# Hybrid decoder block on one core: the mixer's normalised input kept on chip as high and low halves, every mixer projection in three float32r products

## Reference

```python
h = rmsnorm(x, norm_mix_g)
q, k, v, xr, yr, ga, gl = split_cols(h @ w_in)      # 512,128,128,512,512,1024,1024 columns
y_attn = sliding_window_attention(rope(q), rope(k), v, sinks) @ w_attn_o    # window 128, 8 blocks
xr = causal_depthwise_conv(xr, conv_w, conv_b)
y_lru = (rg_lru(xr, ...) * gelu(yr)) @ w_lru_o      # recurrence over positions
x = x + (sigmoid(ga) * y_attn + sigmoid(gl) * y_lru) @ w_out
h = rmsnorm(x, norm_ffn_g)
x = x + moe(h, ...)                                 # top 4 of 32 experts, clamped SwiGLU
return rmsnorm(x, norm_final_g)
```

## Time and profile before

| what | us |
|---|---|
| median of 3 runs | 2228.98 (2228.72 to 2231.96) |
| the profiled execution, and its span | 2230.49, 2228.9 |
| first branch product / last | 26.4 / 136.5 |
| block-diagonal products until | 150.3 |
| attention's project(3) starts | 211.4 |
| gates and projections | 353.5 to 641.7 |
| first product of w_out | 648.9 |
| experts' loop | from about 810 |

### The profile page before, as it was taken

One profiled execution on the slowest core, in us unless ns is written; L12 is line 12 of the kernel. 1 busy time (PEld: TensorE's weight loads), 2 busy tenths in 40 slices (PEclk: granted clock), 3 DMA queues, 4 the chain that ended last, 5 costly groups with the idle time before them and its releaser, 6 DMA issues.

```text
span 2228.9 us, 36027 instructions
## 1 busy us (share of the span) xinstructions
PE 2088.0 (94%) x11352; PEld 1494.9 (67%) x11353; DVE 1550.9 (70%) x1964; ACT 1244.1 (56%) x1655; POOL 291.4 (13%) x334
## 2 busy tenths in 40 slices
PE   7989988999989749999999999999999999999993
PEld 4445555767668637777777777777777777777772
DVE  4326654555443448878877778987877998977894
ACT  3152434334333336766766657766766776765674
POOL 3010000000002420211212200111210110220000
PEclk9998999999999869999999999999999999999997
DMA  7110020110143476988988779978979979977994
GB/s 225 38 38 0 22 76 1 38 39 1 38 151 133 142 196 224 371 284 287 377 282 282 256 260 380 373 270 291 370 259 325 372 276 368 356 258 246 378 342 159
DMA packets 247678, 489.51 MB, mean 220 GB/s; under 512 B 19915, under 2 KB 29991, under 8 KB 247536
## 3 DMA queue, kind: packets, MB, share of 16 engines
q1 hardware_dynamic: 218768, 439.37, 54.7%
q0 software_dynamic: 21088, 49.35, 8.4%
q10 hardware_dynamic: 7776, 0.19, 0.2%
HBM read 461.01 MB, written 32.05 MB: 221 GB/s over the span
## 4 chain that ended last, share of the span: by engine, by line
PE 84%; DVE 5%; issue 4%; ACT 2%; DMA 2%; SPq 1%; POOL 0%; ACTq 0%; DVEq 0%; POOLq 0%
PE psum L650 14%; PE psum L651 14%; PE psum L654 14%; PE psum L667 8%; PE psum L423 5%; PE psum L548 5%; PE psum L536 3%; PE psum L538 3%; PE psum L531 3%; PE psum L638 2%; PE psum L447 2%; PE psum L491 2%; PE psum L593 1%; PE psum L617 1%; PE psum L594 1%
## 5 line engine op out<-in xcount | busy, mean ns | idle before, releaser
L1451 DVE TENSOR_TENSOR w_lo<-ring,w_hi 128x1024 fp32r<-128x1024 f32 x768 | 915.0, 1221 | 144.2 <-ACT w_hi L890 132.7
L890 ACT ACTIVATE w_hi<-ring 128x1024 fp32r<-128x1024 f32 x768 | 803.7, 1059 | 277.7 <-PE psum L654 269.0
L650 PE MATMUL psum<-w_hi,rows_hi 128*128 128x512 f32 x1024 | 422.6, 413 | 4.3 <-DVE rows_lo L1455 2.5
L651 PE MATMUL psum<-w_hi,rows_lo 128*128 128x512 f32 x1024 | 400.4, 391 | 0.0
L654 PE MATMUL psum<-w_lo,rows_hi 128*128 128x512 f32 x1024 | 316.6, 390 | 0.0
L650 PEld LDWEIGHTS psum<-w_hi,rows_hi 128*128 128x128 f32 x1024 | 194.1, 190 | 47.0 <-issue 10.5
L654 PEld LDWEIGHTS psum<-w_lo,rows_hi 128*128 128x128 f32 x1024 | 192.7, 188 | 41.3
L650 PE MATMUL psum<-w_hi,act_hi 128*128 128x512 f32 x512 | 219.9, 429 | 0.0
L651 PEld LDWEIGHTS psum<-w_hi,rows_lo 128*128 128x128 f32 x1024 | 193.5, 189 | 37.7
L651 PE MATMUL psum<-w_hi,act_lo 128*128 128x512 f32 x512 | 202.7, 396 | 0.0
L667 PE MATMUL psum<-ring,region_m 128*32 128x256 f32 x3072 | 174.2, 380 | 0.0
(11 more groups left out here) (286 smaller groups left out, 2596.0 us busy)
## 6 DMA issues: line engine op xcount, KB each, us to landing
ring<-in_w_gate_up_dram SPq DMA_DIRECT2D x128, 2048.0 KB, 15.9
ring<-in_w_down_dram SPq DMA_DIRECT2D x64, 2048.0 KB, 12.0
ring<-in_w_in_dram SPq DMA_DIRECT2D x9, 1024.0 KB, 8.2
ring<-in_w_in_dram SPq DMA_DIRECT2D x3, 2048.0 KB, 22.6
region_m<-in_x_dram SPq DMA_DIRECT2D x8, 512.0 KB, 9.7
ring<-in_w_out_dram SPq DMA_DIRECT2D x2, 2048.0 KB, 7.7
region_a<-in_x_dram POOLq DMA_DIRECT2D x8, 512.0 KB, 4.8
acc_rows<-region_a POOLq DMA_DIRECT2D x8, 512.0 KB, 2.9
```

Of the source, the lines that this page charges most:

```text
L650: mm(bank(i), hi[:, ks], wh, start=(k0 + q == 0), stop=False)
L651: mm(bank(i), lo[:, ks], wh, start=False, stop=False)
L890: act.activation(w_hi[:, n % NBUF, :], place[i][:, k0 * HALF:(k0 + 2) * HALF], ACT.Copy).then_inc(hi_done, 1)
L1451: v.tensor_tensor(out=w_lo[:, n % NBUF, :], in0=place[i][:, k0 * HALF:(k0 + 2) * HALF], in1=w_hi[:, n % NBUF, :].bitcast(f32), op=ALU.subt ...
```

## The change

The mixer is rebuilt up to w_out; the experts' part and its weights' places stay.

- The input is kept as hT_hi (a ScalarE copy to float32r from the transposes' banks) and hT_lo (a VectorE subtraction), without the norm's gain; the gain goes into the weights, which are also split: ScalarE copies with a scale (`in_high`), VectorE multiplies and subtracts (`in_low`).
- Branches, q, k, v and the two output projections are three float32r products each (`three`).
- x is loaded in two halves with the first branch weights between. TensorE starts the branches after four tiles and does one group between each two of the other tiles' transposes. The groups' order is by token half first.
- ScalarE's 13 constant loads stand behind the eighth tile, and before the first copies out of the branch banks.
- Weights for k and v are loaded when eight branch groups are done, those for q when sixteen are, gates two groups ahead.
- The decay moves into step 1 of the attention loop on both engines, the recurrences into steps 1 and 2. The attention's output oT now lies on `igate`, so ScalarE waits for all recurrences before its first copy of pT. kT goes round four blocks.
- In the gates hT needs no splitting. In the projections oT and lruT are split in 16 pieces of 512 tokens for each group (`out_high`, `out_low`), in `OBUF` = 3 buffers.
- `bias_part` moves into the w_out steps 1 to 5, its loads behind the last projection.

```diff
 # sync
-            sp.dma_start(wq_sb, ...).then_inc(wq_in, 16)
-            sp.dma_start(wkv_sb, ...).then_inc(wkv_in, 16)
-            sp.wait_ge(branch_mm, 8)
+            tiles(0, NT // 2)
             sp.dma_start(wxr_sb, w_in_v[:, :, OFF_XR:OFF_XR + LW]).then_inc(wxr_in, 16)
+            tiles(NT // 2, NT)
             sp.dma_start(wyr_sb, w_in_v[:, :, OFF_YR:OFF_YR + LW]).then_inc(wyr_in, 16)
+            sp.wait_ge(branch_mm, 8)
+            sp.dma_start(wkv_sb, w_in_v[:, :, OFF_KV:OFF_KV + 2 * KVW]).then_inc(wkv_in, 16)
+            sp.wait_ge(branch_mm, 16)
             sp.dma_start(wq_sb, w_in_v[:, :, OFF_Q:OFF_Q + QW]).then_inc(wq_in, 16)
...
 # tensor
+            def three(dst, w_hi_, w_lo_, m_hi_, m_lo_, first, final):
+                mm(dst, w_hi_, m_hi_, start=first, stop=False)
+                mm(dst, w_hi_, m_lo_, start=False, stop=False)
+                return mm(dst, w_lo_, m_hi_, start=False, stop=final)
+
+            def branch(n):
+                w, m, th = n // 8, n % 4, n // 4 % 2
+                hi, lo = ((wxr_hi, wxr_lo), (wyr_hi, wyr_lo))[w]
+                if m == 0 and w == 0:
+                    pe.wait_ge(hT_lo_done, 4 * (th + 1))
+                if n >= 4:
+                    pe.wait_ge(branch_out, n - 3)
+                cols, toks = slice(m * P, (m + 1) * P), slice(th * HALF, (th + 1) * HALF)
+                for k in range(KD):
+                    if n % 8 == 0:
+                        pe.wait_ge(in_lo_done, w * KD + k + 1)
+                    last = three(bank(4 + n % 4), hi[:, k, cols], lo[:, k, cols], hT_hi[:, k, toks], hT_lo[:, k, toks],
+                                 k == 0, k == KD - 1)
+                last.then_inc(branch_mm, 1)
+
+            for t in range(NT // 2):
+                turn_x(t)
+            for t in range(NT // 2, NT):
+                branch(t - NT // 2)
+                turn_x(t)
+            for n in range(4, 16):
+                branch(n)
...
+                    three(bank(1)[:, 0:2 * KVW], h_, l_, wkv_hi[:, k, :], wkv_lo[:, k, :], k == 0, k == KD - 1)
...
+                    last = three(bank(0), h_, l_, wide[0], wide[1], k == 0, k == KD - 1)
...
+                    for q in range(2):
+                        cols = slice(q * P, (q + 1) * P)
+                        for th in range(2):
+                            mm(bank(2 * th + q), hi[:, cols], hT_hi[:, k, th * HALF:(th + 1) * HALF], start=first, stop=False)
...
-                for th in range(2):
-                    for q, (w, x_) in enumerate(((wao_sb, oT), (wlo_sb, lruT))):
-                        for k in range(GROUP):
-                            last = mm(bank(4 + 2 * th + q), w[:, k, j * P:(j + 1) * P], x_[:, k, th * HALF:(th + 1) * HALF],
+                for k in range(GROUP):
+                    for q in range(2):
+                        r = (j * GROUP + k) * 2 + q
+                        lo = (wao_lo, wlo_lo)[q][:, k, j * P:(j + 1) * P]
+                        for th in range(2):
+                            p_ = 2 * r + th
+                            pe.wait_ge(o_lo_done, p_ + 1)
+                            last = three(bank(4 + 2 * th + q), ow_hi[r % 2], lo, o_hi[p_ % OBUF], o_lo[p_ % OBUF],
+                                         k == 0, k == GROUP - 1)
+                            last.then_inc(o_mm, 1)
...
 # scalar
+            for t in range(NT // 2):
+                square(t)
+                if t >= 1:
+                    hT_high(t - 1)
+            hT_high(NT // 2 - 1)
+            act.wait_ge(gmix_in, 16)
+            in_high(wxr_hi, wxr_sb, wxr_in)
+            for t in range(NT // 2, NT):
+                square(t)
+                hT_high(t)
             with nc.allow_non_contiguous_dma("small vectors, one element per partition"):
                 for dst, src in loads:
                     act.dma_start(dst, src).then_inc(consts_in, 16)
+            for n in range(4):
+                branch_copy(n)
+            in_high(wyr_hi, wyr_sb, wyr_in)
...
+                if s == 1:
+                    decay()
                 if s >= 2:
                     b = s - 2
+                    if b == 0:
+                        act.wait_ge(lru_done, LM)
...
+            def out_high(p_):
+                r, th = p_ // 2, p_ % 2
+                j, k, q = r // 8, r // 2 % 4, r % 2
+                if p_ >= OBUF:
+                    act.wait_ge(o_mm, p_ - OBUF + 1)
+                if th == 0:
...
+                    act.activation(ow_hi[r % 2], (wao_sb, wlo_sb)[q][:, k, j * P:(j + 1) * P], ACT.Copy)
+                act.activation(o_hi[p_ % OBUF], (oT, lruT)[q][:, k, th * HALF:(th + 1) * HALF], ACT.Copy).then_inc(o_hi_done, 1)
...
+                for p_ in range(16 * j, 16 * j + OBUF):
+                    out_high(p_)
+                act.wait_ge(gate_mm, KD * (j + 1))
...
+                for p_ in range(16 * j + OBUF, 16 * (j + 1)):
+                    if p_ == 16 * j + 14 and j + 1 < KD:
+                        gate_high((j + 1) * KD)
+                        gate_high((j + 1) * KD + 1)
+                    out_high(p_)
 # vector
+            def out_low(p_):
...
+                    v.tensor_tensor(out=(wao_lo, wlo_lo)[q][:, k, cols], in0=(wao_sb, wlo_sb)[q][:, k, cols],
+                                    in1=ow_hi[r % 2].bitcast(f32), op=ALU.subtract)
+                v.tensor_tensor(out=o_lo[p_ % OBUF], in0=(oT, lruT)[q][:, k, th * HALF:(th + 1) * HALF],
+                                in1=o_hi[p_ % OBUF].bitcast(f32), op=ALU.subtract).then_inc(o_lo_done, 1)
...
-                if s < LM:
-                    recur(s)
+                if s == 1:
+                    decay()
+                    recur(0)
+                    recur(1)
+                if s == 2:
+                    recur(2)
+                    recur(3)
                 if s >= 1:
                     b = s - 1
...
                 if t + 2 < NT:
                     merged_low(t + 2)
+                if 1 <= t <= 5:
+                    bias_part(t - 1)
```

More of the change, by code:

```diff
@@ L30 @@
 FILL = 16
+OBUF = 3
 FAR = 4096
@@ L164, in hybrid_decoder_block, with pieces @@
         pT = take(2 * GROUP * P)
+        bd = pT.rearrange("p (g m n) -> p g m n", g=2, m=LM)
+        cos, sin = (take(NT * 32).rearrange("p (t d) -> p t d", t=NT) for _ in range(2))
+        squares, ang, turn = region_a[:, 0:D], unit_view(region_a[:, D:D + NT * 32], NT), unit_view(region_a[:, D + NT * 32:D + 2 * NT * 32], NT)
+        a2 = prob[0].rearrange("p h k -> p (h k)")
         at[0] = 0
         sgate = [[take(HALF) for _ in range(2)] for _ in range(2)]
[L168 to L183, removed]
+        def pieces(name, count, width):
+            col = at[0]
+            take(count * width)
+            return [over(f"{name}{n}", [P, width], at_a, col + n * width)[:] for n in range(count)]
+        g_hi = pieces("g_hi", 2, 2 * P)
+        o_hi, o_lo = pieces("o_hi", OBUF, HALF), pieces("o_lo", OBUF, HALF)
+        ow_hi = pieces("ow_hi", 2, P)
+        bstage = half_slot(4, 2)[:, 0:3 * D]
+        wo_lo = [over(f"wo_lo{q}", [P, UNIT], at_ring, (4 + q) * UNIT) for q in range(2)]
+        wo_hi = [over(f"wo_hi{q}", [P, UNIT], at_ring, (6 + q) * UNIT) for q in range(2)]
         m_hi = [over(f"m_hi{q}", [P, KD, P], at_s, 1536 + q * D) for q in range(2)]
@@ new lines, in _ @@
+            hT_low(NT // 2 - 1)
+            in_low(wxr_lo, wxr_sb, wxr_hi)
+            for t in range(NT // 2, NT):
+                xnorm(t)
+                hT_low(t)
+            dve.wait_ge(small_built, N_BUILT)
+            dve.wait_ge(consts_in, 16 * N_CONST)
+            then(v.tensor_scalar(clam[:, 2, :], lam[:], -1.0, None, ALU.mult))
+            v.tensor_tensor(out=clam[:, 0, :], in0=lam[:], in1=clam[:, 2, :], op=ALU.max).then_inc(clam_exp, 1)
+            in_low(wyr_lo, wyr_sb, wyr_hi)
@@ new lines, in _, with conv @@
+            then(v.memset(xr[:, :, 0:3], 0.0))
+            def conv(m):
+                dve.wait_ge(branch_out, 5 + m)
+                then(v.tensor_scalar(xc[:, m, :], xr[:, m, 3:3 + SEQ], convw[:, 3, m:m + 1], convb[:, m:m + 1], ALU.mult, ALU.add))
+                for c in (2, 1, 0):
+                    ins = v.scalar_tensor_tensor(out=xc[:, m, :], in0=xr[:, m, c:c + SEQ], scalar=convw[:, c, m:m + 1],
+                                                 in1=xc[:, m, :], op0=ALU.mult, op1=ALU.add)
+                    if c:
+                        then(ins)
+                    else:
+                        ins.then_inc(conv_done, 1)
```

347 lines of the change are left out of this document (167 added, 180 removed).

## The result

The changed kernel takes 2247.77 us (median of 4 runs, 2247.03 to 2248.79), the kernel before beside it 2228.85 (4 runs, 2228.14 to 2231.96): ratio 1.0082, 95% interval 1.0065 to 1.01. It is slower by 0.8%, where 0.6% was forecast; the forecast of 2243.2 is 4.6 us short, and the time lies inside its range. The profiled execution has a span of 2246.2 us.

A forecast was written before the change was run, and what follows sets the result against it. TensorE, busy 94% of the span, was taken as the bound; -0.6 us at the gates' start and +14.9 after gave +14.2, so 2243.2 us from a median of 2228.98, range 2222 to 2264.

The forecast's parts named there:

- Price of a product: Float32r products on TensorE: 0.231 us each, three cost 0.69 against 0.86 for one float32; k and v products 0.12.
- The relief of some 60 us: TensorE over the mixer: cheaper products relieve it of some 60 us in all, including 21.6 for the projections.
- Rival B: Branches, q and gates: a product takes 0.216 as two neighbours share weights; -16 us, 2227; chance 8%.
- Up to the branches: Start to branches' end: branch(0) begins at 22.6, branch(4) at 60.8, branches end at 129.2 instead of 136.5.
- The term of the constant loads: Before branch(4): TensorE waits behind 13 issues on ScalarE's queue, taken as 9 us; the other end is 22.
- rival C: Constant loads keep 22 us (+13), or k and v products cost 0.231 (+18): 2256 to 2261; chance 12%.
- Into the attention: Attention's start: VectorE's serial chain makes project(3) 10.0 us late; five blocks give 10.6 back; gates begin at 352.9.
- Gates: Gates of each column group: the copy and subtraction dropped were covered, so nothing is gained; 21.8 us remain.
- Projections: Output projections, fed by ScalarE and VectorE through 3 buffers: 15.6 against 13.73 us a group, +14.9 for the stage.
- the walk: Projections: all 16 pieces followed through the feed loop, with a 1.7 us wait behind the sigmoids, giving 15.6 us.
- Rivals A and D: Projections: A, feed loop closes at TensorE's pace, 12.7 a group, 2220, 10%; D, TensorE's clock falls, group 20.5, 2293, 8%.
- After: W_out stage: halving unchanged, bias work moved into half-idle VectorE steps costs nothing; 1 to 3 us if cover failed.

The follow-up runs named there:

- loads_early: Changed kernel with ScalarE's 13 constant loads issued in groups of 5, 5 and 3 behind tiles 4, 5 and 6: 2238.64 us, ratio 1.0032.
- gates_hi_w: Changed kernel with the third product of each gate step on high weights, so all load high halves; only gates read: 22.40 us a group.
- gates_lo_w: Changed kernel with all three products of each gate step loading low weights; only gates read: 21.77 us a group.

## Why the prediction came out as it did
- **Price of a product.** 0.231 was taken. The branches show 0.227 (the dense stretch from 69 to 126 us), k and v 0.12 as estimated, the projections' runs without a wait 0.23. A block takes 19.41 us against 19.27 worked out. Rival B's 0.216 did not come: neighbours with the same weights in the gates took 0.232. The Trainium skill ("TensorE: Matmul & The Clock Gate", Back-to-back issue gap) gives 216 ns as the gap of an isolated product; no dense stretch of float32r products here was that fast, the least being 0.227. The relief of some 60 us that was counted does not show in full: TensorE's busy time fell by 36.6. In the gates and projections it fell only from 286.2 to 284.0 us, where 21.6 had been counted, since a group's gates take 0.49 more and its projections are recorded busy 13.0 us, not the 11.1 of 48 products at 0.231.
- **Up to the branches.** branch(0) at 22.54 (22.6). The term of the constant loads was 7.9 us of issues instead of 9, and the block-diagonal products began 2.9 us before the 129.2 of the prediction; loads_early gives the term's share in the end, 7.0. The other end, 22 us, for which rival C stood, did not come. The prediction's reason was that the issues of the kernel before ran beside the weight loads. The rows agree in part: its slow ones, 2.92 to 3.46 us, stood where the DMA moved 341 to 387 GB/s, and here it moved 5 to 34. But three of its issues took only 0.38 to 0.78 between 18.35 and 20.24, where the DMA already moved 396, and no run tells what made the others slow.
- **Into the attention.** Each link of VectorE's chain has the length that was worked out: decay 10.2, recurrences 9.4 and 9.4, softmax 9.85, rotation 3.0. project(3) was 2.6 us earlier than predicted only because the chain began that much earlier. From there to the gates 8.7 came back instead of 10.6: the five blocks gave some 10 (19.41 us each instead of 21.40), and the stretch behind them took about 1 longer. So the forecast of the gates' start, right within 0.7 us, owes that to two misses against each other.
- **Gates.** This is the term that was mis-sized: "nothing is gained, 21.8 us remain". They took 413.99 - 391.69 = 22.3 us, 0.232 a product against 0.227 in the earlier trace rows, at the same granted clock of 1.00. Seven full groups make 3.4 us, more than the whole 2.4 that the forecast was short at the head of w_out (16.6 against 14.2); the stages before it were 0.7 better, and the start of this one 0.7. The other 2.2 of the 4.6 us between the medians lie behind (0.7 behind the head of w_out) and in the runs' own spread.
- **Projections.** 15.6 predicted, 15.63 measured; the wait at the fourth piece was 1.31 instead of 1.7, so the other terms of the walk were 0.4 short together, and the total hides it. With the gates' 0.49 a group is 2.39 us longer where 1.85 was forecast. The last group and the merges cost 2.9 us (665.54 - 641.73 against 648.92 - 628.00), with 1.85 - 0.4 + 1.5 forecast. Rivals A and D are excluded by the windows (all eight groups at a granted clock of 1.00, seven of 15.62 to 15.64 us): 12.7 us was wanted for the one, a clock below 1.00 for the other.
- **After.** From the first w_out product to the end it is 1580.7 us instead of 1580.0, within the 1578.9 to 1581.7 of the runs above; bias_part cost nothing that shows.

Sum to the head of w_out: -1.3 at the gates' start (forecast -0.6), -1.7 for the stage's shorter start, 7 x 2.39, and 2.9, together 16.6; forecast 14.2.

## What to carry to other kernels
Fewer cycles on the busiest engine can be worth less than nothing where its operands must first be made by other engines through a short ring of buffers: here a group's projections took 22.3, 15.6 and 14.8 us with 2, 3 and 4 buffers, and 13.7 with the dear products that need no feeding. Work out that loop, its signals included, and divide by the buffers before trading a dear product for three cheap ones. Small DMA issues and a long serial piece of another engine can be free or cost nearly their full length, depending on what stands behind them in the program; moving them gave 7 and 11 us. The three costs here lay one behind another and added up within 0.3 us, so each could be measured alone.

## What was not expected of the hardware
- Products of the same form and type take 0.227 us in one place and 0.232 in another at the same granted clock; with low halves alone as weights in the gates it was 0.227. Not explained.
- At the start of the gates, after the same wait of 1.83 us, the granted clock was 0.67 in the changed kernel and 0.65 in gates_hi_w, but 1.00 in gates_lo_w. The windows of 4.5 us, in that order:

```profile
352.00:356.50 4.50, 4.34 (x13) 3.50 (x14) 0.41 (x2) 0.05 (x1) 0.00 (x0) 0.67 0.00 0
```

```profile
351.30:355.80 4.50, 4.50 (x14) 3.54 (x14) 0.08 (x1) 0.42 (x1) 0.00 (x0) 0.65 0.00 0
```

```profile
351.20:355.70 4.50, 4.34 (x19) 3.67 (x20) 0.89 (x3) 0.51 (x1) 0.00 (x0) 1.00 0.00 0
```

  The first group's gates say the same of the other runs: in all twelve profiles of changed kernels with high halves as weights they took 23.9 to 24.0 us, and 21.84 in gates_lo_w. So the moment alone is unlikely; but there is only one profile with low halves, and the cause is open.
- TensorE at 13.01 of 15.63 us busy kept its full clock, and at 12.94 of 22.30 it kept it in six groups and lost it in two.
